# Later keys and convolution branch of a two-block layer kernel: 512-column matmuls with the halves added by GpSimd, on one core

## The reference

```python
n = rmsnorm(h, g_mix[l])
proj = n @ w_in[l]
(b_gate, c_gate, h_conv, q, k_c, v_c, k_s, v_s, k_w, v_w,
 g_br, g_conv, g_attn) = jnp.split(proj, split_pts, axis=-1)
u = c_gate * h_in                                   # h_in is h_conv
up = jnp.pad(u, ((0, 0), (CONV_WIDTH - 1, 0), (0, 0)))
conv = sum(up[:, k:k + S, :] * conv_w[k] for k in range(CONV_WIDTH))
y_conv = (b_gate * conv) @ w_out
```

## Time and profile before

| | us |
|---|---|
| median of 3 runs | 743.83 |
| lowest, highest | 743.76, 748.2 |
| the profiled execution's own time | 744.02 |
| its span, first to last instruction | 742.3 |
| PE busy | 736.6 |
| DVE busy | 518.4 |
| ACT busy | 414.4 |
| GpSimd (POOL) busy | 69.1 |

### The profile page before, as it was taken

One profiled execution on the slowest core, in us unless ns is written; L12 is line 12 of the kernel. 1 busy time (PEld: TensorE's weight loads), 2 busy tenths in 40 slices (PEclk: granted clock), 3 DMA queues, 4 the chain that ended last, 5 costly groups with the idle time before them and its releaser, 6 DMA issues.

```text
span 742.3 us, 11516 instructions
## 1 busy us (share of the span) xinstructions
PE 736.6 (99%) x4529; PEld 636.9 (86%) x4529; DVE 518.4 (70%) x834; ACT 414.4 (56%) x786; POOL 69.1 (9%) x104
## 2 busy tenths in 40 slices
PE   8999999999999999999999999999999999999998
PEld 7999999877788888888888888888888888888886
DVE  6685767786756777886467758898668777457762
ACT  6376656456454366555455547697646656346640
POOL 5600000000010000520000005400100000000000
PEclk9999999999999999999999999999999999999999
DMA  8999354253355647757655562735345655656511
GB/s 284 282 290 311 72 149 130 99 172 111 115 170 201 203 150 220 202 188 229 208 173 185 176 222 60 255 114 193 108 154 171 207 191 181 217 170 195 202 57 57
DMA packets 99210, 131.26 MB, mean 177 GB/s; under 512 B 5358, under 2 KB 79164, under 8 KB 99157
## 3 DMA queue, kind: packets, MB, share of 16 engines
q1 hardware_dynamic: 96180, 125.32, 53.0%
q0 software_dynamic: 2304, 4.43, 2.7%
q10 hardware_dynamic: 672, 0.79, 0.3%
HBM read 128.68 MB, written 1.84 MB: 176 GB/s over the span
## 4 chain that ended last, share of the span: by engine, by line
PE 96%; DVE 2%; ACT 1%; issue 0%; POOL 0%; DVEq 0%; POOLq 0%
PE B L1639 38%; PE B L1605 22%; PE B L1610 11%; PE B L1594 11%; PE B L1845 2%; PE B L1892 2%; PE B L1855 2%; DVE LO L1010 1%; PE B L1652 1%; PE B L1730 1%; PE B L1646 1%; PE B L1848 1%; PE B L1872 1%; ACT HI L546 1%; PE B L1775 1%; PE B L1831 0%
## 5 line engine op out<-in xcount | busy, mean ns | idle before, releaser
L1010 DVE TENSOR_TENSOR LO<-RAW,HI 128x1024 fp32r<-128x1024 f32 x236 | 282.7, 1237 | 95.7 <-ACT HI L546 95.1
L1639 PE MATMUL B<-HI,AA 128*128 128x512 f32 (+1 forms) x928 | 280.5, 379 | 0.3 <-DVE AA L1016 0.2
L546 ACT ACTIVATE HI<-RAW 128x1024 fp32r<-128x1024 f32 (+2 forms) x240 | 237.1, 1038 | 64.8 <-PE B L1639 57.9
L1639 PEld LDWEIGHTS B<-HI,AA 128*128 128x128 f32 x928 | 170.6, 188 | 32.9 <-issue 1.1
L1605 PE MATMUL B<-AA,HI 128*128 128x512 f32 x704 | 179.2, 393 | 0.0
L1639 PE MATMUL B<-LO,AA 128*128 128x512 f32 (+1 forms) x464 | 173.9, 375 | 0.0
L1605 PEld LDWEIGHTS B<-AA,HI 128*128 128x128 f32 x704 | 126.7, 189 | 23.0 <-issue 0.7
L1610 PEld LDWEIGHTS B<-AA,LO 128*128 128x128 f32 x704 | 96.6, 190 | 7.2
L1639 PEld LDWEIGHTS B<-LO,AA 128*128 128x128 f32 x464 | 87.5, 189 | 14.7
L1610 PE MATMUL B<-AA,LO 128*128 128x256 f32 x704 | 98.8, 282 | 0.0
L1594 PE MATMUL B<-AA,HI 128*128 128x256 f32 x448 | 83.1, 286 | 0.0
(11 more groups left out here) (314 smaller groups left out, 641.0 us busy)
## 6 DMA issues: line engine op xcount, KB each, us to landing
RAW<-in_w_in SPq DMA_DIRECT2D x29, 1024.0 KB, 5.9
RAW<-in_w_gate SPq DMA_DIRECT2D x22, 1024.0 KB, 5.3
RAW<-in_w_up SPq DMA_DIRECT2D x22, 1024.0 KB, 5.3
RAW<-in_w_down SPq DMA_DIRECT2D x22, 1024.0 KB, 5.0
RAW<-in_w_in SPq DMA_DIRECT2D x9, 512.0 KB, 6.3
RAW<-in_w_attn_out SPq DMA_DIRECT2D x4, 1024.0 KB, 5.1
RAW<-in_w_o SPq DMA_DIRECT2D x4, 1024.0 KB, 5.0
RAW<-in_w_out SPq DMA_DIRECT2D x4, 1024.0 KB, 5.1
```

Of the source, the lines that this page charges most:

```text
L546: e.activation(pieces(HI, NSPL, i, k), pieces(RAW, NRAW, i, k), ACT.Copy).then_inc(split_hi, 1)
L1010: e.tensor_tensor(pieces(LO, NSPL, i, k), pieces(RAW, NRAW, i, k), pieces(HI, NSPL, i, k), ALU.subtract).then_inc(split_lo, 1)
L1639: x = e.matmul(dst, a, w[:, t, c0:c0 + n], start=(first and t == 0 and k == 0), stop=(last and t == nk - 1 and k == 2))
```

## The change

Keys c = 0, 1 of the third branch and the twelve cg, up and bg groups use `both`. ACT copies the whole bank (512 columns) to a pair of `SGC` slots (`parts(g, ...)`, g = 0 to 13), and GpSimd adds the two halves (`summed`): into `KT` for keys, `CG` for cg, and in place for up and bg, where DVE now multiplies from the slot and not from the bank. PE takes a bank again once ACT has copied it. At steps 0, 7 and 12 ACT runs its first fill item ahead of `exponents(i)`; before it did so at step 0 only. The feed-forward parts' semaphores `fg_low` and `fu_low` are renamed to `parts_act` and `up_part`, shared with the new copies, and waited for with 14 and 8 added.

```diff
+        PARTS, SUMS_UP = 14, 8
+        PAIR = [flatten(SGC[:, 2 * k:2 * k + 2, :]) for k in range(4)]
...
@@ gpsimd, behind the DMA bias_rows
+            def summed(g, dst, done):
+
+                e.wait_ge(parts_act, g + 1)
+                e.tensor_tensor(dst, PAIR[g % 4][:, 0:S], PAIR[g % 4][:, S:2 * S], ALU.add).then_inc(done, 1)
+
+            for c in range(2):
+                summed(c, KT[:, 1, c, :], keys_sb)
+            for i in range(2):
+                for c in range(2):
+                    if i == 1:
+                        e.wait_ge(conv_lo, c + 1)
+                    summed(2 + 6 * i + c, CG[:, c, :], cg_sb)
+                for g in range(4 + 6 * i, 8 + 6 * i):
+                    summed(g, PAIR[g % 4][:, 0:S], up_part)
...
@@ scalar
+            def parts(g, done, count, free=None):
+
+                e.wait_ge(done, count)
+                if free:
+                    e.wait_ge(*free)
+                e.activation(PAIR[g % 4], B[g % 2][:, :], ACT.Copy).then_inc(parts_act, 1)
+
             def fill():
                 u = U_FILL
                 hi(u + 2)
                 for c in range(2):
-                    keys(1, c)
+                    parts(c, keys_pe, 3 + c)
                     yield
...
-                        e.wait_ge(cg_pe, 2 * i + c + 1)
-                        if i == 1:
-                            e.wait_ge(conv_lo, c + 1)
-                        e.activation(CG[:, c, :], B[c][:, 0:S], ACT.Copy).then_inc(cg_sb, 1)
+                        parts(2 + 6 * i + c, cg_pe, 2 * i + c + 1, (up_sb, c + 1) if i else None)
                         yield
                     hi(u + 3)
-                    yield
-                    yield
+                    for c in range(2):
+                        parts(4 + 6 * i + c, up_pe, 2 * i + c + 1, (bg_sb, c + 1) if i else (keys_sb, c + 3))
+                        yield
                     hi(u + 4)
-                    yield
-                    convolved(2 * i)
-                    yield
+                    for c in range(2):
+                        parts(6 + 6 * i + c, bg_pe, 2 * i + c + 1, (cg_sb, 2 * i + c + 1))
+                        if c == 1:
+                            convolved(2 * i)
+                        yield
...
             filler = fill()
-            next(filler)
             for i in range(NSTEP + 2):
+                early = i in (0, 7, 12)
+                if early:
+                    next(filler)
                 if i < NSTEP:
                     exponents(i)
-                for _ in range(FILL_AT[i] - (i == 0)):
+                for _ in range(FILL_AT[i] - early):
                     next(filler)
...
@@ vector
-                        e.wait_ge(up_pe, n + 1)
+                        g = 4 + 6 * i + c
+                        e.wait_ge(up_part, 4 * i + c + 1)
                         e.wait_ge(cg_sb, n + 1)
...
-                        e.tensor_tensor(UP[:, c, 2:258], B[c][:, 0:S], CG[:, c, :], ALU.mult).then_inc(up_sb, 1)
+                        e.tensor_tensor(UP[:, c, 2:258], PAIR[g % 4][:, 0:S], CG[:, c, :], ALU.mult).then_inc(up_sb, 1)
...
-                        e.wait_ge(bg_pe, n + 1)
-                        e.tensor_tensor(CG[:, c, :], B[c][:, 0:S], CG[:, c, :], ALU.mult).then_inc(bg_sb, 1)
+                        g = 6 + 6 * i + c
+                        e.wait_ge(up_part, 4 * i + c + 3)
+                        e.tensor_tensor(CG[:, c, :], PAIR[g % 4][:, 0:S], CG[:, c, :], ALU.mult).then_inc(bg_sb, 1)
...
@@ tensor
                 for c in range(2):
-                    keys(U_FILL, 1, c)
+                    take(c, parts_act, c + 1)
+                    both(U_FILL, 128 * c, B[c], 0, c == 0).then_inc(keys_pe, 1)
                     yield
...
-                        take(c, cg_sb, 2 * i + c + 1)
-                        stationary(u, 128 * c, B[c][:, 0:S], 0, c == 0).then_inc(cg_pe, 1)
+                        take(c, parts_act, 3 + 6 * i + c)
+                        both(u, 128 * c, B[c], 0, c == 0).then_inc(cg_pe, 1)
                         yield
                     for c in range(2):
-                        take(c, up_sb, 2 * i + c + 1)
-                        stationary(u + 1, 128 * c, B[c][:, 0:S], 0, c == 0).then_inc(up_pe, 1)
+                        take(c, parts_act, 5 + 6 * i + c)
+                        both(u + 1, 128 * c, B[c], 0, c == 0).then_inc(up_pe, 1)
                         yield
                     for c in range(2):
-                        take(c, bg_sb, 2 * i + c + 1)
-                        stationary(u + 2, 128 * c, B[c][:, 0:S], 0, c == 0).then_inc(bg_pe, 1)
+                        take(c, parts_act, 7 + 6 * i + c)
+                        both(u + 2, 128 * c, B[c], 0, c == 0).then_inc(bg_pe, 1)
                         yield
```

More of the change, by code:

```diff
@@ L195, in program @@
         diag_sb, spread_pe, spread_sb = sem("diag_sb"), sem("spread_pe"), sem("spread_sb")
-        fg_pe, fg_low, fg_sb, normed_sb, silu_sb = (sem(n) for n in ("fg_pe", "fg_low", "fg_sb", "normed_sb", "silu_sb"))
-        fu_pe, fu_low, fu_sb, ff_sb, ff_hi, ff_lo = (sem(n) for n in ("fu_pe", "fu_low", "fu_sb", "ff_sb", "ff_hi", "ff_lo"))
+        fg_pe, parts_act, fg_sb, normed_sb, silu_sb = (sem(n) for n in ("fg_pe", "parts_act", "fg_sb", "normed_sb", "silu_sb"))
+        fu_pe, up_part, fu_sb, ff_sb, ff_hi, ff_lo = (sem(n) for n in ("fu_pe", "up_part", "fu_sb", "ff_sb", "ff_hi", "ff_lo"))
         mean_sb, root_sb, factor2 = sem("mean_sb"), sem("root_sb"), sem("factor2")
@@ L794, in ffn @@
                         e.wait_ge(fg_pe, f0 + f + 1)
-                        e.activation(SGC[:, f % 4, :], B[c][:, S:2 * S], ACT.Copy).then_inc(fg_low, 1)
+                        e.activation(SGC[:, f % 4, :], B[c][:, S:2 * S], ACT.Copy).then_inc(parts_act, 1)
                     if i == 0:
@@ L805, in ffn @@
                         e.wait_ge(fu_pe, f0 + f + 1)
-                        e.activation(SGC[:, 4 + f % 4, :], B[5 + c][:, S:2 * S], ACT.Copy).then_inc(fu_low, 1)
+                        e.activation(SGC[:, 4 + f % 4, :], B[5 + c][:, S:2 * S], ACT.Copy).then_inc(up_part, 1)
                     for c in range(2):
@@ L1335, in ffn @@
                         f = 2 * i + c
-                        e.wait_ge(fg_low, f0 + f + 1)
+                        e.wait_ge(parts_act, PARTS + f0 + f + 1)
                         e.tensor_tensor(SGC[:, f % 4, :], B[c][:, 0:S], SGC[:, f % 4, :], ALU.add).then_inc(fg_sb, 1)
@@ L1345, in ffn @@
                         f = 2 * i + c
-                        e.wait_ge(fu_low, f0 + f + 1)
+                        e.wait_ge(up_part, SUMS_UP + f0 + f + 1)
                         e.tensor_tensor(SGC[:, 4 + f % 4, :], B[5 + c][:, 0:S], SGC[:, 4 + f % 4, :], ALU.add).then_inc(fu_sb, 1)
```

## The result

The changed kernel takes 751.96 us in the median of 6 runs, the kernel before 743.81 of 6 on the same chip: ratio 1.0108, 95% interval 1.0077 to 1.0139. The forecast was 748.2, its range ended at 751.8, so the time lies 0.2 us outside. The direction and the place were right, and the sizes were not. In some executions, of the kernel before too, all that follows the first 20 us comes 4 to 5 us later: in two of the six here, while the other four took 751.18 to 752.21 (median 751.63), and in the profiled ones of experiments 1, 2 and 5.

What follows compares the result with a forecast made beforehand. PE was taken to bound the kernel, so only its matmuls and new waits count. From the profiled 744.02: - 1.3 + 5.0 + 0.7 = + 4.4, so 748.4, or 748.2 against the median; range 742.4 to 751.8.

Steps and rivals of the forecast that it cites:

- What bounds, and that only a wait of PE counts: Whole kernel: PE busy 736.6 of 742.3 us, so only fewer or shorter matmuls and new PE waits move the end.
- The gain of the form: Fourteen groups on PE, each 2.79 us instead of 2.88: 1.26 us gained, bounds 0 and 2.5.
- The gap at bg0: PE waits 5.0 us near 104.6 for unit 17's low half, through late split, copy, sum and `UP`; bounds 4.6 to 5.6.
- The second narrow place: Step 12, first gate group: PE waits 0.7 us for bank 0, freed by ACT's copy behind `hi(22)`; bounds 0 and 1.3.
- DVE, ACT with it, also runs some 0.45 us later: From step 9 on, since the second half's up0 sum comes at 128.82, where the multiplication stood at 128.40.
- rival 3: GpSimd's sums hold DVE up in many places: 2.6 us more, 750.8; chance 0.09, shared with several small waits.
- Against it: 5 us is one gap, and work comes densely on both sides: Argument that PE's clock would not fall after the gap at bg0.
- rival 1: PE's clock falls after the gap at bg0: 1.5 to 3.1 us more, 749.7 to 751.3; chance 0.23.
- the prediction's own sign: In the changed kernel's profile, a gap of 5 us and a granted clock under 1.00 would mean rival 1.
- Rival 2: Unit 18 lands at 97 us or before, so no gap opens at bg0: 742.5 to 743.2; chance 0.14.
- Copies ahead of the exponents, free: Steps 7 and 12: ACT's copy goes before `exponents`, whose results are needed two steps on; no cost.

Runs made afterwards that it cites:

- experiment 1: The changed kernel with ACT's copy of the first up0 bank ahead of the split of unit 18 instead of behind it: 744.8 us, ratio 1.0008.
- experiment 2: The changed kernel with 38 matmuls on constants where PE waits before the first bg0: 753.31 us; refilled with 19 instead: 750.56 us, ratio 1.0086.
- experiment 5: experiment 1 plus the second half's first bg copy put ahead of the split of unit 22: 743.1 us, ratio 0.9988.
- experiment 6: The kernel before with the fourteen groups in the 512- and 256-column form, without copies or sums, part of the result left out: 743.28 us, ratio 0.9996.
- experiment 4: The kernel before with one wait added, DVE's first UP multiplication also waiting for ACT's split of unit 18: 749.63 us, ratio 1.0078.
- experiment 3: The changed kernel with GpSimd's transfer of the bias rows issued behind the fourteen sums: 752.38 us, ratio 1.0122.
- experiment 10: The changed kernel with 8 matmuls on constants ahead of the wait at the first bg0 group: 751.19 us, ratio 1.0094.
- experiment 7: experiment 5 without the copies ahead of the exponents at steps 7 and 12 (at step 0 only): 742.89 us, ratio 0.9982.

## Why the prediction was right and wrong

- **What bounds, and that only a wait of PE counts:** right. PE's two waits and the low clock that the first one brought are the whole loss.
- **The gain of the form, 14 x 0.09 = 1.26 us:** nearly. The trace gives 0.46 and 0.49 for six groups each and 0.07 a group in experiment 6, so about 0.08, 1.1 in all.
- **The gap at bg0, 5.0 us:** right in its place, its chain and each link; 4.40 measured. The sum took 0.73 (0.74 taken). Unit 18 landed at 101.41 in this execution, 0.7 earlier than in the profile before, and bg0 started at 109.09, 0.6 before the 109.66 forecast; that is the difference. Experiment 1 shows that the gap hangs on the order, experiment 4 that the late `UP` alone is enough for one, experiment 3 the bias transfer behind the landing.
- **The second narrow place, 0.7 us:** mis-sized, 1.4 measured. The mechanism, ACT's copy behind `hi(22)`, is shown by experiment 5. What failed is the step "DVE, ACT with it, also runs some 0.45 us later": it counted one sum as GpSimd's own time beside a DVE that goes on. That sum took 0.95 us instead of 0.74, and the next one shut DVE out for 0.53 more, which the step put at nothing: 0.74 together, the whole excess. Cutting the two sums took 0.5 and 0.5 off the wait. Their holding of DVE was left out of the sum and kept as rival 3, as without a price in the rows.
- **The clock:** here the forecast fell. The step was "Against it: 5 us is one gap, and work comes densely on both sides", which made rival 1 worth 0.23 and the clock at 1.00 the likeliest case. The sum had no term for the clock, that is 0 us. The clock fell, and the refilled gap of experiment 2 puts its cost at 2.4 us, inside the 1.5 to 3.1 of the rival; the shorter low stretches of experiments 4 and 10, 3.4 us each, cost 1.4 and 1.6. By the prediction's own sign, a gap and a clock under 1.00, this is rival 1. The rule of the Trainium skill ("TensorE: Matmul & The Clock Gate", section "Why this matters for your kernels") that was cited beside it held: a gap of microseconds brings the lower level, here one of 4.15 us. The trace of before had no gap of this kind, so its rows spoke neither way, and the density of the work around was taken for evidence against. The price was read from the start of the trace by its pace alone; the granted clock reads 1.00 there too, so the half pace at the start is not shown by that number.
- **The range:** each rival was priced with all other terms at their middle. The clock and a second wait of 1.4 came together. With the measured terms the sum closes: 744.02 - 1.1 + 4.4 + 2.4 + 1.4 = 751.1, the profiled 751.18. The median is 0.8 above that execution. Later landings of unit 18 (102.64 and 102.84 in the profiles of experiments 2, refilled, and 4) could make part of it, but that wasn't measured. That the time fell just outside the range, and not just inside, is chance: the executions lie on both sides of its end.
- **Rival 2** (the gap doesn't open) did not come. Its time, 742.5 to 743.2, is that of experiments 5 and 7 (743.1 and 742.89), without either wait; experiment 1, with the wait at step 12 left, took 744.8. The gain is real once no copy that PE needs waits behind a split.
- **Rival 3** (the sums hold DVE up): its mechanism is there, in one place that reaches PE, and is worth 0.7 us, not 2.6. The sums at 115.26 and 121.13 took 1.27 us each too, with no wait of PE behind them.
- **Copies ahead of the exponents, free:** right, on the kernel with both orders turned (experiment 7).

## What to carry to other kernels

When an engine that works off a fixed list gets a new urgent duty, look at what stands ahead of it on that list, and at when that thing is ready: here a copy of 0.6 us cost 7 us because it stood behind a split whose weights came 34 us after their issue. If a change opens a gap of a few microseconds on a PE that was never idle, price the lower clock with it as part of the same case, not as a separate rival: here it added 1.4 to 2.4 us where PE had stood still for 2.9 to 4.2. And a GpSimd instruction beside DVE is not free because GpSimd is idle: here its sums and DVE's split of two SBUF inputs waited for each other in full.

## What the runs showed of the hardware

- The granted clock fell to 0.50 at idle times of PE of 2.91, 3.57, 4.15 and 5.93 us (experiments 10 and 4, the changed kernel, experiment 3), and was back after 3.4, 3.4, 6.8 and 6.8 us. In the shortest case it fell at 109.98, 0.2 us after PE had started again, in the three others while PE was still idle. At an idle time of 1.26 us (the gates, changed kernel) it stayed 1.00.
- One 768 KB DMA from GpSimd's queue that writes the bias rows takes 34 to 36 us in both places tried, and a 1 MB weight unit issued beside it lands after 34 and 29 us instead of 5 to 6.
- A float32 matmul of 128 columns makes two records, 0.22 us together; 38 calls took 8.5 us.
- GpSimd's addition of 256 columns takes 0.73 us with DVE out of the way and up to 1.81 beside it; one of a single column beside DVE ends 0.04 to 0.05 us after DVE's instruction, in three cases.
